# Low parts of the weights: computed in every quarter, or computed once, stored to DRAM and loaded

## The reference, cut to what matters

```python
h = rmsnorm(x, g_norm);  z = h @ w_in                       # 1024 x 2312
att = sliding-window attention (window 128, 8 query heads, 2 kv heads, sinks, relative bias)
hm  = mLSTM, 4 heads of 64 x 128 state, chunkwise, with running-max stabiliser
x = x + concat(rmsnorm(att), per-head rmsnorm(sigmoid(o) * hm)) @ w_out       # 1024 x 1024
x = x + relu(rmsnorm(x) @ w_up)**2 @ w_down                 # 1024 x 4096, 4096 x 1024
y = rmsnorm(x, norm_final)
```

## Time and profile before

| | before |
|---|---|
| median of three runs | 2769.32 us (2766.51 to 2775.98) |
| the profiled execution | 2771.24 us, span 2769.1 us |
| mean granted TensorE clock | 0.937 |
| PE, PEld busy | 2507.2 us (91%), 2085.8 us (75%) |
| DVE busy | 1369.2 us (49%), of it 438.0 us in L900, the low parts of the weights |
| ACT busy | 893.2 us (32%), of it 365.2 us in L559, their high parts |
| DMA | 224.29 MB, mean 81 GB/s; 189.82 MB of it on SP's queue |

### The profile page before, as it was taken

How to read it: one execution, slowest core, us unless ns; L and a number is a source line. 1 busy time by engine, 2 the same in 40 slices (tenths; PEclk the granted TensorE clock), 3 DMA queues, 4 the chain that set the end, 5 groups by cost and what they waited for, 6 DMA issues and landing times. The chain is left out here.

```text
span 2769.1 us, 32194 instructions
## 1 busy us (share of the span) xinstructions
PE 2507.2 (91%) x12867; PEld 2085.8 (75%) x12867; DVE 1369.2 (49%) x2705; ACT 893.2 (32%) x1638; POOL 51.9 (2%) x88
## 2 busy tenths in 40 slices
PE   6888899999889799999889799999987688999995
PEld 5776688887776688887776688888875568888884
DVE  4475544445475444445475444445374435444442
ACT  3342423233343323233353323233333213222321
POOL 2000000000000000000000000000012000000000
PEclk9999899999999899999999899999995598999998
DMA  5211132334211122334211132334211221222221
GB/s 172 69 46 46 61 98 92 92 110 160 77 46 47 61 91 96 95 107 160 76 46 50 57 96 92 99 107 152 72 47 30 26 64 54 84 77 77 77 83 47
DMA packets 181841, 224.29 MB, mean 81 GB/s; under 512 B 22027, under 2 KB 132660, under 8 KB 181676
## 3 DMA queue, kind: packets, MB, share of 16 engines
q1 hardware_dynamic: 165596, 189.82, 22.3%
q10 hardware_dynamic: 12000, 24.94, 2.6%
q0 software_dynamic: 4096, 7.47, 1.3%
HBM read 210.78 MB, written 12.60 MB: 81 GB/s over the span
## 5 line engine op out<-in xcount | busy, mean ns | idle before, releaser
L1542 PE MATMUL ps<-a_hi,w_hi 128*128 128x512 f32 (+1 forms) x1640 | 585.2, 357 | 29.1 <-DVE a_lo L904 16.8
L1544 PE MATMUL ps<-a_hi,w_lo 128*128 128x512 f32 (+1 forms) x1640 | 586.9, 358 | 0.0
L1543 PE MATMUL ps<-a_lo,w_hi 128*128 128x512 f32 (+1 forms) x1640 | 585.5, 357 | 0.0
L559 ACT ACTIVATE w_hi<-w_raw 128x1024 fp32r<-128x1024 f32 (+2 forms) x368 | 365.2, 1032 | 650.3 <-PE ps L1544 584.8
L900 DVE TENSOR_TENSOR w_lo<-w_raw,w_hi 128x1024 fp32r<-128x1024 f32 (+2 forms) x368 | 438.0, 1199 | 205.6 <-ACT w_hi L559 205.4
L1542 PE MATMUL ps<-w_hi,u_hi 128*128 128x512 f32 (+1 forms) x1088 | 430.8, 396 | 10.5 <-DVE x L904 10.5
L1543 PE MATMUL ps<-w_lo,u_hi 128*128 128x512 f32 (+1 forms) x1088 | 427.5, 393 | 0.0
L1544 PE MATMUL ps<-w_hi,u_lo 128*128 128x512 f32 (+1 forms) x1088 | 427.1, 393 | 0.0
L1542 PEld LDWEIGHTS ps<-a_hi,w_hi 128*128 128x128 f32 x1640 | 314.0, 191 | 75.2 <-DVE a_lo L904 18.2
L1543 PEld LDWEIGHTS ps<-a_lo,w_hi 128*128 128x128 f32 x1640 | 311.9, 190 | 44.2
L904 DVE TENSOR_TENSOR x<-x,ps 128x512 f32<-128x512 f32 x272 | 185.4, 686 | 322.5 <-PE ps L1544 322.1
(11 more groups left out here) (289 smaller groups left out, 2083.2 us busy)
## 6 DMA issues: line engine op xcount, KB each, us to landing
w_raw<-in_w_up_dram SPq DMA_DIRECT2D x128, 512.0 KB, 3.7
w_raw<-in_w_down_dram SPq DMA_DIRECT2D x128, 512.0 KB, 3.5
w_raw<-in_w_out_dram SPq DMA_DIRECT2D x32, 512.0 KB, 4.2
w_raw<-in_w_in_dram SPq DMA_DIRECT2D x24, 580.0 KB, 3.9
w_raw<-in_w_in_dram SPq DMA_DIRECT2D x24, 512.0 KB, 3.7
x<-in_x_prompt_dram ACTq DMA_DIRECT2D x16, 512.0 KB, 6.5
w_raw<-in_w_in_dram SPq DMA_DIRECT2D x32, 256.0 KB, 2.9
wide<-in_x_prompt_dram ACTq DMA_DIRECT2D x12, 512.0 KB, 4.2
```

The lines of the kernel that those rows point to most:

```text
L559: eng.activation(w_hi[b][:, k * n:(k + 1) * n], raw[p % RAW][:, 0:n], ACT.Copy).then_inc(w_high.sem, 1)
L1542: eng.matmul(out, lh, rh, start=(k == ks[0]), stop=False)
L1543: eng.matmul(out, lh, rl, start=False, stop=False)
L1544: ins = eng.matmul(out, ll, rh, start=False, stop=(k == last))
```

## The change

`w_lo` is computed by VectorE in quarter 0 only. SP stores each unit's low part to an internal DRAM tensor `low_dram` (one row of up to 9280 bytes for each partition), after the raw loads of the unit after it. In quarters 1 to 3 SP loads it from there straight into `w_lo`, after the raw loads of the same unit and after TensorE has finished unit u - 2. The raw tiles then come free by ScalarE's copy alone (`w_high`), and TensorE waits for `w_high` and the landing. Some signals are merged (`bias_vec`, `bias_moved`, `kwin_vec`), which changes no order of work. The core of the diff:

```diff
+        low_dram = nc.dram_tensor("w_lo_units", [UNITS, P, WMAX], F32, kind="Internal").ap()
...
-        w_split = signal("w_split", PIECES, RAW)
+        w_split = signal("w_split", 0)
+        lo_stored = [signal(f"lo_stored{b}", 0) for b in range(UNIT_BUFS)]
+        lo_landed = [signal(f"lo_landed{b}", 16 * (UNITS // UNIT_BUFS), -16 * (UNITS // UNIT_BUFS)) for b in range(UNIT_BUFS)]
...
+        def unit_used(eng, q, u):
+
+            if u >= UNIT_BUFS:
+                unit_done(eng, q, u - UNIT_BUFS)
+            elif q:
+                unit_done(eng, q - 1, u - UNIT_BUFS + UNITS)
...
+            def raw_free(q, p):
+
+                if q == 0:
+                    if p >= RAW:
+                        sp.wait_ge(w_split.sem, w_split.at(0, p + 1 - RAW))
+                elif p >= RAW:
+                    sp.wait_ge(w_high.sem, w_high.at(q, p + 1 - RAW))
+                elif q == 1:
+                    sp.wait_ge(w_split.sem, w_split.at(0, PIECES + p - RAW + 1))
+                    sp.wait_ge(w_high.sem, w_high.at(1, p + 1 - RAW))
+                else:
+                    sp.wait_ge(w_high.sem, w_high.at(q, p + 1 - RAW))
+
+            def unit_low(q, u):
+
+                n = unit_shape(u)[0] * unit_shape(u)[1]
+                b = u % UNIT_BUFS
+                if q == 0:
+                    sp.wait_ge(w_split.sem, w_split.at(0, 2 * u + 2))
+                    sp.dma_start(low_dram[u, :, 0:n], w_lo[b][:, 0:n].bitcast(F32)).then_inc(lo_stored[b].sem, 16)
+                else:
+                    if q == 1:
+                        sp.wait_ge(lo_stored[b].sem, lo_stored[b].at(0, 16 * UNITS // UNIT_BUFS))
+                    unit_used(sp, q, u)
+                    sp.dma_start(w_lo[b][:, 0:n].bitcast(F32), low_dram[u, :, 0:n]).then_inc(lo_landed[b].sem, 16)
+
             def load(q, p, src, shift=0):
...
-                sp.wait_ge(w_split.sem, w_split.at(q, p + 1 - RAW + shift))
+                raw_free(q, p)
...
+            def low_after(q, u):
+
+                if q == 0:
+                    if u:
+                        unit_low(0, u - 1)
+                else:
+                    if q == 1 and u == 0:
+                        unit_low(0, UNITS - 1)
+                    unit_low(q, u)
...
             def split_act(eng, q, last, u, k, i=0):
...
+                    unit_used(eng, q, u)
...
             def split_vec(eng, q, u, k, i=0):
+                if q:
+                    return
...
+                if k == 0 and u >= UNIT_BUFS:
+                    eng.wait_ge(lo_stored[b].sem, lo_stored[b].at(0, 16 * (u // UNIT_BUFS)))
                 eng.wait_ge(w_high.sem, w_high.at(q, p + 1 + 16 * i))
...
             def unit_ready(q, u, i=0):
-                eng.wait_ge(w_split.sem, w_split.at(q, 2 * (u + 1) + 16 * i))
+                if q == 0:
+                    eng.wait_ge(w_split.sem, w_split.at(0, 2 * (u + 1)))
+                else:
+                    eng.wait_ge(w_high.sem, w_high.at(q, 2 * (u + 1)))
+                    eng.wait_ge(lo_landed[u % UNIT_BUFS].sem, lo_landed[u % UNIT_BUFS].at(q, 16 * (u // UNIT_BUFS + 1)))
```

More of the change, by code:

```diff
@@ L315, in hymba_layer, with unit_done @@
             chunk_parity[U_M + 2 * n] = chunk_parity[U_M + 2 * n + 1] = c % 2
+        def unit_done(eng, q, u):
+            last = q == NQ - 1
+            T, tiles, splits = tokens_of(last)
+            NT, NN = len(tiles), len(splits)
+            kind, n, w = unit_of(u)
+            if kind == "F":
+                eng.wait_ge(fm_out.sem, fm_out.at(q, NN * sum(len(t) for t in FM_TILES[:n + 1])))
+            elif kind == "T":
+                eng.wait_ge(tm_out.sem, tm_out.at(q, NT * (n + 1)))
+            elif kind == "O":
+                eng.wait_ge(op_out.sem, op_out.at(q, NT * (n + 1)))
+            else:
+                kind, c, half = mlp_unit(n)
+                if kind == "U":
+                    eng.wait_ge(up_out.sem, up_out.at(q, 4 * NN * c + 2 * NN * (half + 1)))
+                else:
+                    eng.wait_ge(dn_out.sem, dn_out.at(q, 2 * NT * c + NT * (half + 1)))
+        def unit_used(eng, q, u):
[3 more added lines that the diff above has]
+                unit_done(eng, q - 1, u - UNIT_BUFS + UNITS)
         block = ctx.enter_context(nc.Block())
@@ L381, in quarter @@
                         constants_in()
+                    low_after(q, u)
                 p = 2 * U_M
@@ L387, in quarter @@
                             p += 1
+                        low_after(q, p // 2 - 1)
             for q in range(NQ):
@@ L446, in _ @@
         def _(pool):
-            pool.wait_ge(bias_sb.sem, 1)
-            pool.dma_start(bias_line, bias_by_distance).then_inc(bias_out.sem, 16)
+            pool.wait_ge(bias_vec.sem, bias_vec.at(0, 1))
+            pool.dma_start(bias_line, bias_by_distance).then_inc(bias_moved.sem, 16)
             pool.memset(bias0[:, :, :], MASKED).then_inc(bias0_made.sem, 1)
-            pool.wait_ge(bias_out.sem, 16)
-            pool.dma_start(bias_dram, bias_line.unsqueeze(1).broadcast_to([H, P, 3 * P])).then_inc(bias_spread.sem, 16)
-            pool.wait_ge(bias_spread.sem, 16)
+            pool.wait_ge(bias_moved.sem, bias_moved.at(0, 16))
+            pool.dma_start(bias_dram, bias_line.unsqueeze(1).broadcast_to([H, P, 3 * P])).then_inc(bias_moved.sem, 16)
+            pool.wait_ge(bias_moved.sem, bias_moved.at(0, 16 * 2))
             for h in range(H):
                 src = bass.AP(bias_dram.tensor, h * 3 * P * P + P - 1, [[3 * P - 1, P], [1, 2 * P]])
-                pool.dma_start(bias[:, h, :], src).then_inc(bias_in.sem, 16)
+                pool.dma_start(bias[:, h, :], src).then_inc(bias_moved.sem, 16)
             for dst, src in ((kwin_sample, cache_k_win), (vwin_sample, cache_v_win)):
@@ L523, in _ @@
         def _(eng):
[L524 to L540, removed]
             def split_act(eng, q, last, u, k, i=0):
@@ L546, in split_act @@
                 if k == 0:
-                    before = u - UNIT_BUFS
-                    if u == 0 and not (isinstance(q, int) and q == 0):
-                        unit_used(eng, q - 1, last, UNITS - 2, 0)
-                    elif u == 1:
-                        eng.wait_ge(dn_out.sem, dn_out.at(q, 0))
-                    elif before == U_M + 1 and not isinstance(i, int):
-                        unit_used(eng, q, last, before, 0)
-                        eng.wait_ge(dn_out.sem, dn_out.at(q, 4 * len(tokens_of(last)[1]) * i))
-                    elif u > 1:
-                        unit_used(eng, q, last, before, i)
+                    unit_used(eng, q, u)
                 b = u % UNIT_BUFS
```

33 lines of the change are left out of this document (16 added, 17 removed).

## The result

The changed kernel takes 2774.8 us (median; 2768.8 to 2783.3) against 2768.9 us of the kernel before in the same runs: ratio 1.0019 [1.0011, 1.0027]. A second set of runs, beside the experiments, gave 2772.2 against 2769.8 us, 1.0003 [0.9991, 1.0016]. So the medians are 5.9 and 2.5 us slower where 2 us faster was forecast; the second interval doesn't exclude no change. The range of 2752 to 2780 us held it, and it is within 0.3%. Of the 20 runs of the first set one slow run of 4957 us is left out of the spread. The profiled execution of the changed kernel took 2771.06 us, near the lowest of its runs and 0.2 us under the profiled one of before (2771.24 us), so this pair of traces shows nothing of the median's loss as a whole, only how it is made up.

A forecast was written before the change was run, and what follows sets the result against it. TensorE, 91% busy, was taken as the bound, with VectorE's work mostly under its cover. Gains of 9.9 us less costs of 7.4 us gave 2.5 us net from 2768.7 us; forecast 2766.8 us after 1.9 us for the runs' median, range 2752 to 2780.

The forecast's parts named there:

- Heads' low parts: Heads' stretch, quarters 1 and 2: without VectorE's split, the third block's low part is ready in time; 2.8 us gain.
- Last quarter's O steps: VectorE would read the second step at once, removing TensorE's 3.7 us wait and 1.7 us half-clock loss: 5.4 us gain.
- L1609's block: Attention, before block 3 of quarter 1: exponentials were late by 1.00 us behind VectorE's split; 1.0 us gain in all.
- MLP's loads: MLP: each 1 MB low-part load takes 4.6 us, has 11.1 us, and so costs nothing under cover of TensorE.
- Quarter 0: Quarter 0: the added stores push raw pieces back in the F units; 0.5 us cost, bounds 0 and 3.
- Units 3 and 6: Quarters 1 and 2: low parts ready later, 1.7 us each at unit 3, 0.9 at unit 6; costs 3.4 and 1.8 us.
- one such stretch for the two quarters: F units, quarters 1 and 2: unit 3's longer wait brings one half-clock stretch in all, costing 1.7 us.
- The sum of costs: Unit 3's waits 3.4, unit 6's 1.8, half clock 1.7 and quarter 0's stores 0.5 us: 7.4 us.
- own signs of being wrong: A `w_lo` wait in the MLP, units 3 to 6 waiting over 5 us a quarter, or 712 to 866 us shortening over 3.
- Late low parts: Rival: at units 3, 5 and 6 of later quarters 1 MB loads take 7 us; 2784 us, chance 0.17.
- VectorE as the pace: Rival: VectorE sets the attention's pace, so half-clock stretches go in quarters 1 to 3; 2757 us, chance 0.22.
- The third: Rival: raw loads were the limit, so the removal buys nothing and quarter 3's 5.4 us is lost; 2772 us, chance 0.08.

The follow-up runs named there:

- e1_again: The changed kernel run once more with no edit, for a second trace and more times; 2772.2 us against 2769.8 us for the kernel before.
- e1_both: Changed kernel with VectorE's subtraction put back in quarters 1 to 3, written over the raw piece, loads kept; 2786.8 us, ratio 1.0057 to the kernel before.
- e1_neither: Changed kernel without loads or subtraction in quarters 1 to 3, so leftover low parts are used; 2758.1 us, ratio 0.9956 to the kernel before.
- e1_f_vec: Changed kernel, but VectorE makes low parts of units 0 to 6 in every quarter, neither stored nor loaded; 2762.1 us, 0.9970 to the kernel before.
- e2_mlp_loads: Changed kernel, but only the 32 MLP units' low parts are stored and loaded, VectorE makes units 0 to 13; 2775.6 us, 1.0014.
- e2_u3_vec: Changed kernel, but unit 3's low part is made by VectorE in every quarter, neither stored nor loaded; 2771.0 us, ratio 1.0001 to the kernel before.
- e2_u36_vec: Changed kernel, but low parts of units 3 and 6 are made by VectorE in every quarter, neither stored nor loaded; 2762.7 us, 0.9969.
- e3_x_late: Changed kernel, but ScalarE asks for x blocks one by one in the attention blocks, not at the quarter's start; 2752.2 us, 0.9939.
- e3_before_x_late: Kernel before the change, with x blocks asked for one by one in the attention blocks; 2761.1 us, ratio 0.9972.
- e3_mix_x_late: Changed kernel, only low parts of units 8 to 13 stored and loaded, x blocks asked for in the attention blocks; 2750.2 us, 0.9938.
- e2_mix_loads: Changed kernel, but only low parts of units 8 to 13 are stored and loaded, VectorE makes the others; 2763.5 us, 0.9978.
- e3_u6_x_late: Changed kernel with x blocks asked for in the attention blocks and unit 6's low part made by VectorE in every quarter; 2752.9 us, 0.9943.

## Why the prediction was wrong

- *Removed work: right.* Heads' low parts 2.8 us forecast, 2.9 measured in quarters 1 and 2. Last quarter's O steps 5.4, measured 4.8. L1609's block 1.0, measured 1.1. In sum 9.9 and the 3.9 us of waits for L900, 13.8; the two comparisons with the loads held fixed give 14.6 and 11.7 us.
- *What the removal gives back: put at nothing, and a term that failed.* The MLP quarters are 0.9 and 0.7 us longer wherever the O units' pair is gone, with or without MLP loads. TensorE idles longer in one piece at the norm before them (the longest a_lo wait is 5.1 us, it was 4.2 and 4.4), and the first stretch of the MLP at half clock grows from 3.9 and 4.3 us to 5.9 and 5.7. The mLSTM stages of quarters 1 and 2 together are 3.1 us longer in after and 1.7 us in e1_again. That is 3 to 5 us together; how much of the mLSTM part is chance is open (last section).
- *MLP's loads: right.* 4.8 us for 1 MB, no wait, and e1_both shows the price to be zero. Quarter 0: 0.2 us where 0.5 was taken.
- *Units 3 and 6: place and waits right, price of the clock too small.* Forecast 3.2 us at unit 3, measured 2.9 and 3.0; unit 6 1.5, measured 1.8 and 0.7. The low part of unit 3 was forecast for 690.3 us and landed at 690.2. "I take one such stretch for the two quarters: 1.7 us" failed: both waits were followed by one. Against before, the F stretches are 6.3 us longer in after and 5.9 in e1_again, where 6.9 was in the sum: the second stretch at half clock is made up for by quarter 3, 1.3 us shorter, where nothing was forecast.
- *The cost of the loads as a whole: the other failed term.* The sum of costs, 7.4 us and the 3.9 of L900, makes 11.3 us; e1_neither and e1_both put it at 14.1 and 17.0. The first alone isn't clear of 11.3 by the intervals of the ratios, the second is (12 to 19 us). Of the 3 to 6 us missing, the F stretches of the traces hold 1.2 to 1.5 (12.0 and 12.3 us for the loads, where the sum had 10.8), about the second stretch at half clock. The stores were looked for in quarter 0 only; those at its end reach into quarter 1 and keep F 1 at 55.7 to 55.9 us in e1_f_vec and e2_mlp_loads, without any F load in it. In after they don't add to the F loads' wait at unit 3 (2.9 us against 3.0 in quarter 2, which has no store). The rest, 2 to 4 us, is in the medians and not located in a trace.
- *None of the prediction's own signs of being wrong appeared.* No wait for `w_lo` stands in the MLP, units 3 to 6 wait under 5 us in a quarter (4.7 and 3.7), and the stretch from the first T unit to the heads isn't over 3 us shorter (1.7 us longer in quarter 1, 1.9 shorter in quarter 2). The places were right; the forecast of a gain hung on a net of 2.5 us between sums of 9.9 and 7.4, which the two failed terms outweigh.
- *The burst was taken as fixed.* The prediction counted unit 2's and unit 3's low parts in one line of bytes behind y, x and the raw pieces, which is why its wait was right. It didn't ask which of these could wait. e2_u3_vec and e2_u36_vec show that VectorE in place of the load of unit 3 leaves the wait, and e3_x_late that taking x away removes it with all loads in place. By the medians the same change is worth 2761.1 - 2752.2 = 8.9 us without the burst and costs 2.5 to 6 us with it. Of this turn of 11 to 15 us the F stretches of the traces hold 4.0 us (after is 6.3 us longer than before there with the burst, 2.3 without); where the rest is stays open.
- *The rivals.* Late low parts (2784 us) asked for 7 us for 1 MB; it was 4.8 us, 8.3 in the burst, and the waits grew by a third of what that rival gave. VectorE as the pace: the attention stretches moved by 1.1 us at most, and the one stretch at half clock that is gone in after (attention of quarter 2) is there in e1_again. The third fell with the O steps. In the median a load of 1 MB landed in 4.8 us, in the burst in 8.3. The Trainium skill, "DMA: Bandwidth & Descriptors" (Bandwidth, Measured), gives 6.15 us of DMA time for 1 MB, in a table for DMAs issued from GpSimd; the trace, with SP issuing, doesn't agree where the engines aren't full: 4.8 us from issue to landing.

## What to carry to other kernels

Before traffic is added to a kernel, list what else the DMA engines carry in the one stretch where they are full, and how soon each of those transfers is needed: moving what is needed latest out of it can decide the sign of the change, as the medians have it here. Test which transfer is late by leaving each one out, for a wait named after one operand can stay when that operand isn't loaded at all. Look also at what the test puts in its place: here a subtraction behind a late raw piece, which kept TensorE as long. A wait of 3 us in these traces has to be priced with the stretch of half clock behind it. A forecast of 0.1%, the difference of two sums three and four times as large, says little about the sign.

## What the runs showed of the hardware

In the F units of quarters 1 and 2 each of the twelve waits of TensorE of 2.3 to 4.3 us, in all kernels, had a stretch of at least 3.4 us at the lower level of the clock begin in it or within 1.2 us of its end. Waits of up to 2.0 us had none, nor had two of 2.5 us in quarter 3 (e3_before_x_late, e3_mix_x_late).

The same mLSTM stage of quarters 0 to 2 took 55.5 to 55.8 us in 32 of the 42 cases of the fourteen traces, with 10.2 us at the lower level of the clock. In five it took 56.4 to 56.5 us, with 13.4 to 13.7 us at it (e1_again twice, e1_f_vec, e2_mix_loads twice), and in five 58.6 to 58.7, with 14.7 to 18.6 (after's quarter 1, e2_u3_vec's quarter 0, two quarters of e1_neither, one of e3_u6_x_late). Eight of these ten are among the 20 stages in which VectorE makes no low parts, two among the 22 in which it does. So the removal seems to make them likelier; with so few it isn't shown, and one and the same kernel has both lengths. Runs of before and after spread over 8 to 15 us, those of e3_x_late and e2_u36_vec over 2. It doesn't go with the waits in the F units alone: e2_u36_vec has waits of 2.3 and 3.2 us there, and e3_mix_x_late, without them, spreads over 7.

A raw piece of 512 KB landed in 3.7 us in the median of before, 5.1 with a 1 MB load on the same queue, and 6.4 to 8.5 in the burst. The store of 1 MB took 6.4 us where the load took 4.8.
